# A mixture-of-experts block on one Trainium2 core: the experts' second bias added in the passes instead of by a product with the gates

## The chip, the cores and the metric

The kernel runs on one core of one Trainium2 chip. The metric is the time of one execution on the device in microseconds. Five instruction streams run side by side and meet at semaphores: TensorE (PE in the profile, its weight loads PEld), VectorE (DVE), ScalarE (ACT), GpSimd (POOL), and SyncE (SP), which here only issues DMAs.

## The reference, cut to what matters

All is float32. 1024 tokens of 1024 channels go through a mixing layer (convolution and attention), which gives `h`; then every token is sent to 4 of 32 experts:

```
v = rms_norm(h, norm2_g)
logits = v @ router_w + router_b
top_val, top_idx = lax.top_k(logits, 4)
gates = softmax(top_val)
...
def clamped_swiglu_expert(xb, w1, b1, w2, b2):
    h = xb @ w1 + b1
    x_glu = jnp.minimum(h[..., :D_FF], SWIGLU_LIMIT)
    x_lin = jnp.clip(h[..., D_FF:], -SWIGLU_LIMIT, SWIGLU_LIMIT)
    act = x_glu * jax.nn.sigmoid(SWIGLU_ALPHA * x_glu) * (x_lin + 1.0)
    return act @ w2 + b2
...
y = h + sum over the 4 experts e of a token: gate_e * expert_e(v)
```

So the second bias comes into a token's output as the sum of `gate_e * b2[e]` over its four experts.

## The kernel before, in words

**Mixing** takes the first 380 us of the span: convolution on VectorE, attention, and their projections on TensorE. It is not touched.

**Routing** goes over eight tiles of 128 tokens. Its order is written out by hand per engine, as a loop over `t` in which each engine does a piece of tile t, of tile t-1 and of tile t-2. For tile t TensorE multiplies by `w_out` in two halves (`out_half`, L1215); VectorE adds x and gets the residual tile `hb` (`residual`, L830); ScalarE squares and sums it (L596), POOL makes the root (L335, L336), and VectorE scales the tile into `vrow` (`norm_v`, L838). TensorE transposes `vrow` (L1288), ScalarE copies that (L604), TensorE multiplies by the router's weights (L1307), and VectorE picks four experts and makes the gates (`route`, L843 to L858), which stand in the last 32 columns of `vrow`. Then, two tiles behind, comes the second bias: TensorE transposes the gates (`trans_gates`, L1259), ScalarE copies them (`take_GT`, L613), TensorE multiplies them by the table of all 32 bias rows (`gates_b2`, L1269, two products of 512 columns), and VectorE adds the two halves to `hb` (`add_b2`, L864) and gives `h2_ready`. For that semaphore SP waits before it stores `hb` to the output (`store_rows`, L239), and TensorE before it reuses the banks (L1265, L1280). The row store of `vrow` to `token_rows` is issued ahead of it.

After the last tile TensorE counts ranks within experts (L1318), VectorE makes from them positions and tables (L878 to L968), and POOL gathers the tokens of the first pass from `token_rows` (`gather`, L314).

**Expert passes.** A pass has one expert and up to 256 of its token slots; there are 32 with these inputs. Passes are sorted by how many slots are filled. 18 are narrow (up to 128), then come 14 wide ones, in code of its own for each width (136, 144, 152, 176, 192 here). In `pe_pass` TensorE makes eight blocks of the hidden layer (L1001, each with its two sides), then the second layer: in a narrow pass straight into rows of tokens (`down_rows`, L1041), in a wide one transposed (`down`, L1016) and turned back (`trans_y`, L1029, L1030). Between them it transposes the next pass's tokens (`trans_x`, L1335). In `dve_pass` VectorE takes each hidden block out (`hidden_a`, L663 and L665; `hidden_b`, L672 and L675), after the second block prepares the next pass's indices, after the fourth waits for the adds of the pass before and takes over index and gate (L689, L690), and at the end takes the transposed tokens (`take_xT`, L973). The loop's head copies the expert's first bias (L655). In `act_pass` ScalarE copies the result out times the gate, in two column halves (`take_rows`, L454; `take_y`, L443 and L444), and gives `yt_ev` for each. POOL waits for both and adds the rows to the output in HBM by two indirect DMAs (`add_rows`, L320). SP loads the next weights as buffers come free: `w1` in two parts after the fourth and the eighth hidden block, `w2` in two parts after each half of the second layer (L249, L254). All weight buffers are single.

```
for c in range(2):
    sp.wait_ge(hid_mm, q * MT + (4 * c + 4 - MT))
    load_w1(sp, c, e)
for c in range(2):
    sp.wait_ge(y_mm, q * KD + (4 * c + 4 - KD))
    load_w2(sp, c, e)
```

Of the kernel before, what the change touches and what calls it, by code (L numbers as in the profile page):

```python
# [18 lines left out]
P = 128  # L19
# [20 lines left out]
HALF = 512  # L40


def hybrid_block(nc, x, norm1_g, w_in, conv_w, conv_b, conv_ln_g, conv_ln_b, q_norm_g, k_norm_g, sinks,
# [9 lines left out]
    with ExitStack() as ctx:  # L53
# [71 lines left out]
        b2_sb = part(140, D)[0:NE, :]  # L125
# [34 lines left out]
        GT = sb("GT", [NE, P])  # L160
# [54 lines left out]
        gt_mm, gt_ev, b2_mm, h2_ready = sem("gt_mm"), sem("gt_ev"), sem("b2_mm"), sem("h2_ready")  # L215
# [20 lines left out]
        def store_rows(sp, t):  # L236
            sp.wait_ge(gate_ready, t + 1)
            sp.dma_start(rows_d[t * P:(t + 1) * P, :], vrow[:, t % 2, :]).then_inc(row_out[t % 2], 16)
            sp.wait_ge(h2_ready, t + 1)  # L239
            sp.dma_start(out2[t * P:(t + 1) * P, :], hb[:, t % 4, :]).then_inc(h_out[t % 4], 16)  # L240
# [11 lines left out]
        def load_w2(sp, c, e):  # L252
            src = expert(w2, e)
            sp.dma_start(w2_sb[:, :, c * HALF:(c + 1) * HALF],  # L254
                         src[:, c * HALF:(c + 1) * HALF].rearrange("(k p) n -> p k n", p=P)).then_inc(w2_in[c], 16)

        @block.sync
        def _(sp):
# [22 lines left out]
            sp.dma_start(b2_sb, b2).then_inc(b2_in, 16)  # L281
# [10 lines left out]
            for c in range(2):  # L292
                load_w2(sp, c, 0)
            sp.wait_ge(tab_ready, 1)
            n_pass = sp.value_load(tabI[0:1, 4 * TQ:4 * TQ + 1], min_val=NE, max_val=QMAX)
            with sp.Fori(1, n_pass) as q:
# [4 lines left out]
                for c in range(2):  # L301
                    sp.wait_ge(y_mm, q * KD + (4 * c + 4 - KD))
                    load_w2(sp, c, e)

# [19 lines left out]
        def _(pool):  # L324
# [73 lines left out]
            pool.wait_ge(b2_mm, NT)  # L398
# [7 lines left out]
            with pool.Fori(0, n_pass) as q:  # L406
# [4 lines left out]
                pool.wait_ge(yt_ev, q * 2 + 2)  # L411
# [58 lines left out]
        def _(a):  # L470
# [140 lines left out]
            def take_GT(t):  # L611
                a.wait_ge(gt_mm, t + 1)
                a.activation(GT[:], bank[7][0:NE, 0:P], ACT.Copy).then_inc(gt_ev, 1)  # L613

            for t in range(NT + 1):
                if 1 <= t <= NT:
                    take_vT(t - 1)
                if t >= 2:
                    take_GT(t - 2)
# [4 lines left out]
            take_GT(NT - 1)  # L624
# [20 lines left out]
        def dve_pass(v, q, e, e_next, prep, one_hots, take_idx, take_xT):  # L645
# [55 lines left out]
            v.sem_inc(dve_loop, OWN - own[0])  # L701

        @block.vector
        def _(v):
# [155 lines left out]
            def add_b2(t):  # L860
                v.wait_ge(b2_mm, t + 1)
                for b in range(2):
                    t_ = hb[:, t % 4, b * HALF:(b + 1) * HALF]
                    last = v.tensor_tensor(t_, t_, bank[4 + b][:], ALU.add)  # L864
                last.then_inc(h2_ready, 1)

            for t in range(NT + 1):
# [5 lines left out]
                if t >= 2:  # L873
                    add_b2(t - 2)
# [31 lines left out]
            add_b2(NT - 1)  # L906
# [180 lines left out]
        def _(pe):  # L1087
# [168 lines left out]
            def trans_gates(u):  # L1256
                pe.wait_ge(gate_ready, u + 1)
                pe.wait_ge(lvar, 2)
# [138 lines left out]
```

## Time and profile before

| | |
|---|---|
| median of 3 runs | 2150.91 us (2150.83 to 2156.55) |
| the profiled execution's own time | 2154.91 us |
| its span | 2153.2 us |
| TensorE busy | 2020.3 us, 94%, in 13213 records |
| VectorE busy | 932.0 us, 43% |
| ScalarE, POOL busy | 397.5 us, 228.1 us |
| chain that ended last | TensorE 82%, VectorE 10%, issue 3%, ScalarE 2% |
| moved by DMA | 492.44 MB, 229 GB/s over the span |
| mean granted TensorE clock | 0.964 |

The own time has 1.7 us around the span. An f32 product has two records on TensorE, so "x4" of L1269 is two products. In a timeline a row is start, duration, engine, line, operation, operands, count, and in brackets how long the engine was idle before it and what released it; in the chain a row is start, length, and what stood in the chain. Durations of products overlap in the timeline, so the chain's shares are what a product takes of the time.

### The profile page before, as it was taken

Reading aid. Unit: us, or ns where it says so; the run is one execution under the profiler, and the core shown is the slowest. Engines: PE = TensorE matmul, PEld = TensorE weight load, DVE = VectorE, ACT = ScalarE, POOL = GpSimd, SP = SyncE. Lnnn points to the kernel's source line nnn. Section 1 sums busy time; section 2 is a strip of 40 time slices with the busy share of each in tenths; the row PEclk is TensorE's granted clock in tenths of the full one; section 3 lists DMA queues with packets and bytes.
Section 4 is the critical chain, followed back from the end, with each engine's and each line's share of the span. In section 5 each row is a group of like instructions: output and inputs, shape, how many; then the busy total and the mean of one; then the engine's idle time right before and its main releaser. Section 6 shows DMA issues by size and latency. Waiting matters only on the chain.

```text
span 2153.2 us, 34646 instructions
## 1 busy us (share of the span) xinstructions
PE 2020.3 (94%) x13213; PEld 1648.4 (77%) x13214; DVE 932.0 (43%) x2247; ACT 397.5 (18%) x849; POOL 228.1 (11%) x223
## 2 busy tenths in 40 slices
PE   5997887899799999999999999999999999998997
PEld 3444543444677887788878887999999999988997
DVE  2895667333444444444443444333333333333221
ACT  3113334311111111111111111121111111110111
POOL 3101110000101010011101010011000000000000
PEclk9998889998799999999999999999999999999999
DMA  5020003212599899998999899988788887775651
GB/s 224 1 78 0 1 1 134 87 66 99 195 328 336 304 327 329 337 326 305 327 338 332 298 338 328 322 286 300 275 279 275 279 280 260 267 266 166 237 176 41
DMA packets 226274, 492.44 MB, mean 229 GB/s; under 512 B 7469, under 2 KB 8009, under 8 KB 226224
## 3 DMA queue, kind: packets, MB, share of 16 engines
q1 hardware_dynamic: 207504, 431.24, 55.5%
q0 software_dynamic: 16768, 59.98, 10.2%
q8 instruction: 39, 0.64, 0.1%
q10 hardware_dynamic: 1952, 0.49, 0.1%
q14 instruction: 11, 0.09, 0.0%
HBM read 458.88 MB, written 32.80 MB: 228 GB/s over the span
## 4 chain that ended last, share of the span: by engine, by line
PE 82%; DVE 10%; issue 3%; ACT 2%; DMA 1%; POOL 1%; ACTq 0%; DVEq 0%; POOLq 0%
PE bank L1001 46%; PE bank L1041 11%; PE bank L1016 10%; DVE arena L740 5%; PE bank L1215 5%; PE bank L1335 2%; PE bank L1136 1%; PE bank L1120 1%; ACT arena L543 1%; PE bank L1269 1%; PE bank L1029 1%; DVE arena L769 1%; DVE arena L785 1%; DVE mx L774 1%; PE bank L1307 1%
## 5 line engine op out<-in xcount | busy, mean ns | idle before, releaser
L1001 PE MATMUL bank<-arena 128*128 128x128 f32 (+5 forms) x8192 | 998.4, 284 | 21.5 <-issue 21.5
L1001 PEld LDWEIGHTS bank<-arena 128*128 128x128 f32 x8192 | 989.3, 192 | 34.1 <-issue 34.1
L663 DVE TENSOR_SCALAR arena<-bank,b1c 128x256 f32<-128x256 f32 x256 | 123.8, 483 | 611.1 <-PE bank L1001 602.0
L430 ACT ACTIVATE arena<-arena 128x256 f32<-128x256 f32 x256 | 106.6, 417 | 866.7 <-DVE arena L663 784.0
L1041 PE MATMUL bank<-arena 128*128 128x512 f32 x576 | 262.1, 593 | 0.0
L1016 PE MATMUL bank<-arena 128*128 128x144 f32 (+4 forms) x1792 | 252.0, 294 | 4.6 <-DVE arena L675 4.4
L1016 PEld LDWEIGHTS bank<-arena 128*128 128x128 f32 x1792 | 237.1, 190 | 7.8 <-DVE arena L675 7.7
L973 DVE TENSOR_SCALAR arena<-bank,cols 128x256 f32<-128x256 f32 x256 | 112.1, 480 | 283.4 <-PE bank L1335 283.4
L320 POOL DMA_INDIRECT out<-arena,idx_cur x64 | 99.0, 1547 | 826.9 <-ACT arena L444 422.5
L1041 PEld LDWEIGHTS bank<-arena 128*128 128x128 f32 x576 | 102.5, 190 | 94.7 <-issue 90.4
L740 DVE SCALAR_TENSOR_TENSOR arena<-arena,cols 128x1024 f32<-128x1024 f32 x120 | 159.3, 1328 | 3.7 <-ACT arena L518 0.2
L314 POOL DMA_INDIRECT arena<-token_rows,idx_next x66 | 65.5, 992 | 630.7 <-DVE idx_next L899 551.3
L675 DVE SCALAR_TENSOR_TENSOR arena<-arena 128x256 f32<-128x256 f32 x256 | 108.9, 425 | 37.8 <-DVE arena L672 5.2
L1215 PE MATMUL bank<-arena 128*128 128x512 f32 x256 | 121.5, 631 | 3.0 <-DVE arena L822 3.0
L665 DVE TENSOR_SCALAR arena<-bank,b1c 128x256 f32<-128x256 f32 x256 | 121.6, 475 | 0.0
L1120 PE MATMUL bank<-arena 128*128 128x512 f32 x256 | 110.2, 592 | 0.0
L672 DVE TENSOR_TENSOR arena<-arena 128x256 f32<-128x256 f32 x256 | 106.3, 415 | 0.0
L1215 PEld LDWEIGHTS bank<-arena 128*128 128x128 f32 x256 | 50.6, 202 | 67.7 <-issue 63.9
L1120 PEld LDWEIGHTS bank<-arena 128*128 128x128 f32 x256 | 48.5, 190 | 60.3 <-issue 60.3
L1335 PEld LDWEIGHTS bank<-ident,arena 128*128 128x128 f32 x392 | 50.5, 144 | 42.7 <-issue 33.7
L434 ACT ACTIVATE arena<-bank 128x256 f32<-128x256 f32 x112 | 42.9, 383 | 211.3 <-PE bank L1016 211.3
L1335 PE MATMUL bank<-ident,arena 128*128 128x128 f32 x392 | 66.4, 279 | 3.3 <-ACT arena L631 2.9
(222 smaller groups left out, 1108.8 us busy)
## 6 DMA issues: line engine op xcount, KB each, us to landing
arena<-in_w SPq DMA_DIRECT2D x192, 2048.0 KB, 11.9
arena<-in_x SPq DMA_DIRECT2D x16, 512.0 KB, 5.2
token_rows<-arena SPq DMA_DIRECT2D x8, 528.0 KB, 5.9
arena<-in_w_in SPq DMA_DIRECT2D x2, 2048.0 KB, 11.2
out<-arena SPq DMA_DIRECT2D x8, 512.0 KB, 2.9
arena<-in_w_in SPq DMA_DIRECT2D x1, 3072.0 KB, 23.3
arena<-in_w_out SPq DMA_DIRECT2D x1, 2048.0 KB, 9.5
arena<-in_w_out SPq DMA_DIRECT2D x2, 1024.0 KB, 15.6
```

Source lines behind the costliest of these rows:

```text
L430: a.activation(sg[:, m % 2, :], g1[:, m % 2, :], ACT.Sigmoid, scale=ALPHA).then_inc(sg_ready, 1)
L663: v.tensor_scalar(g1[:, r, :], bank[r][:, 0:SLOTS], b1c[:, m:m + 1], LIMIT, ALU.add, ALU.min).then_inc(g1_ready, 1)
L665: v.tensor_scalar(l1[:, r, :], bank[r][:, SLOTS:], b1c[:, MT + m:MT + m + 1], LIMIT + 1.0, ALU.add, ALU.min).then_inc(hid_free, 1)
L675: v.scalar_tensor_tensor(act[:, m, :], l1[:, r, :], 1.0 - LIMIT, tt[:, r, :], ALU.max, ALU.mult).then_inc(act_ready, 1)
L740: link(v.scalar_tensor_tensor(cT[:, c, :], zT[:, c, j:j + SEQ], col(CW + c * WIDTH + j), cT[:, c, :], ALU.mult, ALU.add))
L973: last = v.tensor_scalar(xT[:, k, :], bank[6][:, (k % 2) * SLOTS:(k % 2 + 1) * SLOTS], col(G2 + k), None, ALU.mult)
L1001: last = mm(bank[m % 2][:, side * SLOTS:side * SLOTS + n], w1_sb[:, k, lo:lo + P], xT[:, k, 0:n], start=k == 0, stop=k == KD - 1)
L1016: last = mm(bank[2 + d % 2][:, 0:n], w2_sb[:, m, d * P:(d + 1) * P], act[:, m, 0:n], start=m == 0, stop=m == MT - 1)
L1041: last = mm(bank[4 + b][:], act[:, m, 0:P], w2_sb[:, m, b * HALF:(b + 1) * HALF], start=m == 0, stop=m == MT - 1)
L1120: last = mm(bank[2 * (i % 2) + side][:], w_cv[:, k, lo:lo + P], uT[:, k, h * HALF:(h + 1) * HALF], start=k == 0, stop=k == KD - 1)
L1215: last = mm(bank[mixed_bank(t) + b][:], src, w_o[:, k, b * HALF:(b + 1) * HALF], start=part_ == 0 and i == 0, stop=part_ == 1 and i == CT - 1)
L1335: last = pe.transpose(bank[6][:, (k % 2) * SLOTS + h * P:(k % 2) * SLOTS + (h + 1) * P], gath[:, h, k * P:(k + 1) * P], ident[:])
```

## The change

The gates' transposes, their copies, the products with the bias table and the adds to `hb` are removed. In each pass SP loads the expert's row of `b2` into all 128 partitions (0.52 MB in SBUF from 4 KB in HBM), and VectorE adds gate times that row to the gated result, after ScalarE's copy: four operations of 512 columns, two token halves by two column halves. `y_ready` takes the place of `yt_ev` in POOL's wait, and SP waits for it before it overwrites the row. The residual tile is stored as soon as it is made, ahead of the row store.

```diff
-        b2_sb = part(140, D)[0:NE, :]
+        b2_rows = part(160, D)
...
         def store_rows(sp, t):
+            sp.wait_ge(h_ready, t + 1)
+            sp.dma_start(out2[t * P:(t + 1) * P, :], hb[:, t % 4, :]).then_inc(h_out[t % 4], 16)
             sp.wait_ge(gate_ready, t + 1)
             sp.dma_start(rows_d[t * P:(t + 1) * P, :], vrow[:, t % 2, :]).then_inc(row_out[t % 2], 16)
-            sp.wait_ge(h2_ready, t + 1)
-            sp.dma_start(out2[t * P:(t + 1) * P, :], hb[:, t % 4, :]).then_inc(h_out[t % 4], 16)
...
+        def load_b2(sp, e):
+            src = b2[e:e + 1, :] if isinstance(e, int) else b2[ds(e, 1), :]
+            sp.dma_start(b2_rows, src.to_broadcast([P, D])).then_inc(b2_in, 16)
...
             sp.wait_ge(var_mm, 2)
-            sp.dma_start(b2_sb, b2).then_inc(b2_in, 16)
...
             for c in range(2):
                 load_w2(sp, c, 0)
+            load_b2(sp, 0)
...
                     sp.wait_ge(y_mm, q * KD + (4 * c + 4 - KD))
                     load_w2(sp, c, e)
+                sp.wait_ge(y_ready, q)
+                load_b2(sp, e)
...
-            pool.wait_ge(b2_mm, NT)
...
                 gather(pool, q + 2)
-                pool.wait_ge(yt_ev, q * 2 + 2)
+                pool.wait_ge(y_ready, q + 1)
...
-                if t >= 2:
-                    take_GT(t - 2)
...
                 take_xT(q4, i)
             v.sem_inc(dve_loop, OWN - own[0])
+            v.wait_ge(b2_in, q * 16 + 16)
+            for b in range(2):
+                v.wait_ge(yt_ev, q * 2 + b + 1)
+                for h in range(2):
+                    y = ytok[:, h, b * HALF:(b + 1) * HALF]
+                    last = v.scalar_tensor_tensor(y, b2_rows[:, b * HALF:(b + 1) * HALF], gate_cur[:, h:h + 1], y,
+                                                  ALU.mult, ALU.add)
+            last.then_inc(y_ready, 1)
...
-                if t >= 2:
-                    add_b2(t - 2)
...
-            add_b2(NT - 1)
...
-                    if u >= 2:
-                        pe.wait_ge(h2_ready, u - 1)
...
-                if t >= 2:
-                    trans_gates(t - 2)
...
-                if t >= 2:
-                    gates_b2(t - 2)
...
-            trans_gates(NT - 1)
-            gates_b2(NT - 1)
...
-            pe.wait_ge(h2_ready, NT)
```

On TensorE the last steps of the routing loop, before (the `w_out` products L1215, `vrow`'s transposes L1288, the gates' L1259, the router's L1307, the bias's L1269, the ranks' L1318):

```order
L1215 MATMUL bank<-arena 128x512 x8
L1259 MATMUL bank<-ident,arena 32x128
L1307 MATMUL bank<-rw,arena 128x32 x8
L1269 MATMUL bank<-arena,GT 128x512 x2
L1288 MATMUL bank<-ident,arena 128x128 x8
L1259 MATMUL bank<-ident,arena 32x128
L1307 MATMUL bank<-rw,arena 128x32 x8
L1269 MATMUL bank<-arena,GT 128x512 x2
L1318 MATMUL bank<-Mb,tri_b 128x32
```

And the same place in the change, whose line numbers are lower (L1210 is `w_out`, L1265 the transposes, L1282 the router, L1291 the ranks):

```order
L1210 MATMUL bank<-arena 128x512 x8
L1282 MATMUL bank<-rw,arena 128x32 x8
L1265 MATMUL bank<-ident,arena 128x128 x8
L1282 MATMUL bank<-rw,arena 128x32 x8
L1291 MATMUL bank<-Mb,tri_b 128x32
```

Nothing is left on TensorE between the router's products of one step and the next piece of work; each of the steps before them lost the same two entries.

On VectorE the end of the pass loop, before (the last tokens' L973, then the loop's branch):

```order
L971 REGISTER_ALU
L973 TENSOR_SCALAR arena<-bank,cols 128x256 x2
L983 REGISTER_ALU
L983 COMPARE_AND_BRANCH
```

In the change (L968 is the last tokens', L704 the bias, with a wait at L701 ahead of each pair):

```order
L968 TENSOR_SCALAR arena<-bank,cols 128x256 x2
L701 ISA
L704 SCALAR_TENSOR_TENSOR arena<-arena,gate_cur 128x512 x2
L701 REGISTER_ALU
L704 SCALAR_TENSOR_TENSOR arena<-arena,gate_cur 128x512 x2
L978 REGISTER_ALU
L978 COMPARE_AND_BRANCH
```

The two pairs stand between the last tokens and the branch to the next pass, so the loop's head follows them.

On SP the end of its pass loop in the change (L253 loads `w2`, L258 the bias row):

```order
L253 DMA arena<-in_w 128x8x512
L258 ISA
L258 DMA arena<-in_b 128x1024
L299 REGISTER_ALU
L299 COMPARE_AND_BRANCH
```

The wait and the load come behind the last part of `w2` and ahead of the next pass's `w1`.

## Rows read from the trace of the kernel before

**Rows 1.** The page, DMA busy in tenths in 40 slices of the span

```profile
DMA  5020003212599899998999899988788887775651
```

**Rows 2.** The chain of waits, routing stage: start, length, what

```profile
417.60 0.11 PE bank L1259
...
419.42 1.91 PE bank L1269 x4
...
517.16 2.41 PE bank L1269 x4
519.57 3.71 issue
523.29 1.96 PE bank L1288 x8
...
529.54 3.72 PE bank L1269 x4
...
533.28 1.29 DVE arena L864 x2
...
542.90 6.17 DMA arena<-token_rows,idx_next
```

**Rows 3.** Timeline, end of the routing stage, VectorE and SP

```profile
518.20 0.75 DVE L838 TENSOR_SCALAR arena<-arena,rs 128x1024 f32<-128x1024 f32 x1 [2.12 <-POOL rs L336]
...
521.90 1.28 DVE L864 TENSOR_TENSOR arena<-arena,bank 128x512 f32<-128x512 f32 x2
...
531.73 0.18 DVE L853 CAST Mb<-Mf 128x32 bf16<-128x32 f32 x1
...
541.55 0.34 SPq L240 DMA_DIRECT2D out<-arena  x1
```

**Rows 4.** Timeline, two halves of L1215, and a window (busy times, PEclk, DMA share, GB/s)

```profile
429.10 7.03 PE L1215 MATMUL bank<-arena 128*128 128x512 f32 x16
...
439.79 8.83 PE L1215 MATMUL bank<-arena 128*128 128x512 f32 x16
...
441.00:442.00 1.00, 1.00 (x2) 0.37 (x2) 0.89 (x5) 0.00 (x0) 0.00 (x0) 0.50 0.00 0
```

**Rows 5.** Timeline, the narrow pass that begins at 957.08: VectorE, ScalarE, POOL

```profile
955.51 0.17 DVE L655 COPY b1c<-b1T 128x16 f32 x1 [0.78 <-issue]
960.86 0.48 DVE L663 TENSOR_SCALAR arena<-bank,b1c 128x256 f32<-128x256 f32 x1 [5.17 <-PE bank L1001]
...
964.43 0.48 DVE L663 TENSOR_SCALAR arena<-bank,b1c 128x256 f32<-128x256 f32 x1 [2.70 <-PE bank L1001]
...
973.27 0.16 DVE L689 COPY idx_cur<-idx_next 128x2 int32<-128x2 int32 x1
...
957.37 0.69 ACT L454 ACTIVATE arena<-bank,gate_cur 128x512 f32<-128x512 f32 x1 [6.42 <-PE bank L1041]
...
960.95 1.38 POOL L320 DMA_INDIRECT out<-arena,idx_cur  x1 [0.30 <-issue]
```

**Rows 6.** The instructions of L740: duration in ns, min/median/max

```profile
L740 DVE SCALAR_TENSOR_TENSOR arena<-arena,cols x120: 1273/1285/2173, 64.2 to 340.6; 128x1024 f32<-128x1024 f32 x120
```

**Rows 7.** DMA: issues (KB, us to landing), landing of L320, window of one narrow pass

```profile
arena<-in_w SPq DMA_DIRECT2D x192, 2048.0 KB, 11.9
arena<-in_x SPq DMA_DIRECT2D x16, 512.0 KB, 5.2
...
DMA to landing us min/median/max: 7.2/7.4/9.3
...
957.08:1000.77 43.69, 43.69 (x313) 35.83 (x312) 19.02 (x54) 5.99 (x11) 4.99 (x4) 1.00 0.92 324
```

**Rows 8.** Timeline, a wide pass, and the switch to the 176-wide code

```profile
1823.80 0.68 ACT L444 ACTIVATE arena<-bank,gate_cur 128x512 f32<-128x512 f32 x1
...
1827.93 0.48 DVE L663 TENSOR_SCALAR arena<-bank,b1c 128x256 f32<-128x256 f32 x1 [5.84 <-PE bank L1001]
...
1943.22 7.08 PE L1001 MATMUL bank<-arena 128*128 128x176 f32 x28 [10.01 <-issue]
```

More of the change, by code:

```diff
@@ L159, in hybrid_block @@
         gs = sb("gs", [P, 4])
-        GT = sb("GT", [NE, P])
         Mb = sb("Mb", [P, NT, NE], bf16)
@@ L214, in hybrid_block @@
             "vt_mm", "vt_ev", "lg_mm", "lg_neg", "eg_ready", "gate_ready", "mask_ready"))
-        gt_mm, gt_ev, b2_mm, h2_ready = sem("gt_mm"), sem("gt_ev"), sem("b2_mm"), sem("h2_ready")
+        y_ready = sem("y_ready")
         row_out = [sem(f"row_out{i}") for i in range(2)]
@@ L609, in gate_exp @@
                 a.activation(eg[:], lg[:], ACT.Exp, bias=gs[:, 0:1]).then_inc(eg_ready, 1)
-            def take_GT(t):
-                a.wait_ge(gt_mm, t + 1)
-                a.activation(GT[:], bank[7][0:NE, 0:P], ACT.Copy).then_inc(gt_ev, 1)
             for t in range(NT + 1):
@@ L623, in _ @@
                     gate_exp(t - 1)
-            take_GT(NT - 1)
             for i in range(2):
@@ L858, in route @@
                 v.tensor_scalar(vrow[:, t % 2, D:ROW], gg[:], gs[:, 2:3], None, ALU.mult).then_inc(gate_ready, 1)
[L860 to L865, printed above, removed]
             for t in range(NT + 1):
@@ L1254, in _ @@
             out_half(2, 0)
-            def trans_gates(u):
-                pe.wait_ge(gate_ready, u + 1)
-                pe.wait_ge(lvar, 2)
-                pe.transpose(bank[7][0:NE, 0:P], vrow[:, u % 2, D:ROW], ident[:]).then_inc(gt_mm, 1)
-            def gates_b2(u):
-                if u == 0:
-                    pe.wait_ge(b2_in, 16)
-                else:
-                    pe.wait_ge(h2_ready, u)
-                pe.wait_ge(vt_ev, 2 * min(u + 2, NT))
-                pe.wait_ge(gt_ev, u + 1)
-                for b in range(2):
-                    last = mm(bank[4 + b][:], GT[:], b2_sb[:, b * HALF:(b + 1) * HALF], start=True, stop=True)
-                last.then_inc(b2_mm, 1)
             for t in range(NT + 1):
```

## The prediction

> **What bounds the kernel now.** I read the page first, then the chain of waits, then the timeline of every engine at three places: the eight routed token tiles, one narrow expert pass and one wide one. The DMA slices are at 8 or 9 tenths in nearly the whole expert stage [rows 1]: that asks whether a pass waits for its weights, and it is the first thing to settle, since the change adds transfers there. In the routing stage the chain is TensorE's own work almost without a gap, and the products with the transposed gates (L1269) and their transposes (L1259) stand in it [rows 2]. In the passes it is TensorE again: in a narrow pass VectorE and ScalarE sit idle between their pieces, each waiting for TensorE [rows 5]. So what leaves TensorE in the routing stage is worth its full time, and what VectorE, POOL and the DMA get in the passes costs nothing until it is late for TensorE.
>
> **The change, part by part.**
>
> *Routing stage, steps with five tiles.* Each had a gate transpose (0.11 in the chain) and four records of L1269, which are two f32 products, at 1.91 us; the row at 419.42 stands for the five from 419 to 500 [rows 2]. 5 x 1.91 = 9.6, and six transposes at 0.11 = 0.7: **10.2 us saved**. TensorE stays the bound in a shortened step: the next thing it needs is the normalised tile, and that was ready 1.8 us after L1269 began (518.95 against 517.16 [rows 2, 3]), while in these steps 7 us of L1215 come before it is asked for [rows 4].
>
> *The last steps.* After the sixth pair (517.16, 2.41) TensorE stood 3.71 us, until 523.29 [rows 2]. The normalised tile was ready at 518.20 + 0.75 = 518.95; what TensorE stood for was the wait on h2_ready, given by VectorE's L864 at 521.90 + 1.28 = 523.18 [rows 3]. Both waits go, so the transposes can start at 519.0: 523.3 - 519.0 = **4.3 us saved**, and what is late next is VectorE's L838. Then the pair at 529.54 (3.72) ends at 533.26 [rows 2] while the mask that the rank products wait for (L853) is ready at 531.91 [rows 3]; L864 (533.28, 1.29) ran beside those products. Both gone: 1.35, less a handover, **1.2 us saved**. The eighth pair lay beside VectorE's rank arithmetic, and is worth nothing; so are ScalarE's eight copies of the gates.
>
> *Stores and first gather.* The residual tile is now stored as soon as it is made, before its row store. The gather of the first pass is in the chain with 6.17 us [rows 2], and the last residual store was issued at 541.55, just ahead of it [rows 3]. That store is 0.52 MB; at the 324 GB/s of a pass [rows 7] it takes 1.6. Bounds 0 and 1.6, because the gather's own start-up may have hidden it; I take **0.6 saved**, nearer the lower end, since the store had begun earlier.
>
> *VectorE in the passes.* Four new operations per pass, 128 in all. No row has 128x512 of this form; L740 has it at 1285 ns for 1024 columns [rows 6], so 0.64 to 0.69 each, I take 0.66, with 84 us in all on VectorE. The first pair of a pass runs when TensorE still multiplies. The second waits for the last gated copy, which in the narrow pass ends at 957.37 + 0.69 = 958.06 [rows 5]; the pair ends at 959.4, and the loop's head (0.78 and 0.17 at L655) moves behind it, to 960.35. VectorE's next work came at 960.86, when TensorE's first block was ready, and TensorE needs the result only for its third block, near 964.4 [rows 5]. So 0.5 us are left before anything moves, and some 3 before TensorE does. In the wide pass the copy ends at 1824.48, the pair and the head at 1826.8, and the work comes at 1827.93 [rows 8]. **Cost 0**, cover TensorE's first block; every us beyond the 3 would be paid in each of 31 passes.
> The Trainium skill (Vector Engine (DVE) Microarchitecture Reference, "Points that are easy to get wrong") says this form with two sources in SBUF that aren't bf16 halves throughput. The row of L740 has both sources f32 in SBUF and stands at one column in 1.25 ns, so I don't double it. By that rule, as an estimate, a pair would take 2.6: hidden in the passes, and 1.3 more at the end.
>
> *POOL.* Its adds to the output now wait for y_ready, 1.3 us later. The second was issued at 960.95 and lands 7.4 us on, at most 9.3 [rows 5, 7]; so 969.7 now, or 971.6. VectorE asks for it at 973.27 [rows 5]. Behind POOL's wait there are only the adds and the next pass's gather, which waits for VectorE's words after 973.27 anyway. Cost 0.
>
> *SP and DMA.* The load of the bias row waits for y_ready (959.4) behind the w2 loads; behind it on SP is the next w1 load, which waits for TensorE's fourth block (about 972) anyway. The load is 0.52 MB. Its time on the 16 DMA engines isn't in the trace. Lower end 1.6 us, at the pass's 324 GB/s; upper end 5.2, what a tile of x of that size took from issue to landing [rows 7]. I take 1.6, since transfers queue behind each other here and a latency isn't occupancy. The narrow pass has the engines at 0.92 of 43.7 us: 3.5 us free [rows 7]. It fits, and **costs 0** in 18 narrow passes; the 14 wide ones are longer with the same weights.
> At one place it may not be free: the switch to the 176-wide code, where TensorE stood 10.01 us with nothing recorded [rows 8] while the w2 load ran; I read it as code coming through the same DMA engines. The new load may add to it: 0 to 1.6, I take **0.8 lost**.
>
> *End.* The last add starts a pair later: **1.3 lost**, nothing covers it.
>
> *The clock.* In three of the five steps TensorE's granted clock fell to 0.50, its lower level of 1.2 GHz, for some 3 us, after the stretch of L1307 and L1269, with TensorE busy the whole time; an L1215 group then took 8.83 where 7.03 is usual, 1.8 each, 5.3 in all [rows 4]. The change takes half of that stretch away. Bounds: all 5.3 back, or none and two more falls (-3.6). I take **4.0 saved**, nearer the first, because in two steps of before the same stretch passed without a fall, so it is near the edge.
> The Trainium skill (TensorE: Matmul & The Clock Gate, "Why this matters for your kernels") ties the fall to idle gaps of TensorE. The row shows it at full busy share, so the trace disagrees. By that rule this term would be 0, and the time 4 us higher.
>
> *Sum:* 10.2 + 4.3 + 1.2 + 0.6 - 0.8 - 1.3 = 14.2, and 4.0 of clock: 18.2. Against the profiled execution's own 2154.91 this gives 2136.7; the runs' median is 2150.91, 4.0 lower, from which it would be 2132.7. I can't tell which of the two had the usual number of falls of the clock, so I go between: **2135**.
>
> **The rivals.**
> *The clock falls as often as before* (22 in 100). For it: each step still has the short products of L1307 and eight transposes. 14.2 saved: 2154.9 - 14.2 = 2140.7, or 2136.7 from the median; 2139.
> *A switch of code waits longer* (7 in 100). Its 10.01 stands beside others of a fraction of that, so it isn't stable, and TensorE's code moves in memory. If a second switch gets such a gap, or this one grows by the same: 2135 + 10 = 2145, which counts as no change.
> *The same, shorter* (6 in 100). If it falls to the 1 or 2 us of a plain switch: 2135 - 8 = 2127.
> *The broadcast load is slow: slower than before* (5 in 100). All 128 partitions read one 4 KB row. If the load holds the engines for e us, narrow passes become bound by DMA once e is above the free 3.5, first eating the lead that w1 has over TensorE (its 4 MB are asked for at 972 and needed when the next pass begins at 1000.77, and 11.9 us to landing [rows 7] leave about 16). The gain is gone at 18(e - 3.5) = 16 + 16, e = 5.3; at e = 8 it is 81 - 16 = 65 us lost: 2200. Against it: 5.2 for a whole landing of that size.
> *VectorE comes late: slower too* (3 in 100). It decides when the second pair and the head take more than 3 us above my 2.3. At 1 us beyond that, 31 us: 2166.
>
> **How the numbers follow.** My forecast has 57 in 100. Measurement can tell 0.3%, 6.5 us, from no change: the border is at 2144.4. Forecast, usual clock falls and the shorter switch lie below it: 0.85. The longer switch and the upper edge of the others: 0.08. Slower: 0.07. Range: best ends of the terms from the median, 2150.9 - 21.3 = 2129.6, widened to 2127 for the shorter switch; worst ends from the profiled time, 2154.9 - 12.7 + 3.6 = 2145.8, so 2146. What it leaves out is the two slower cases and part of the switch.
>
> **What would show it.** Right: no idle of TensorE between the routed tiles, a wait of some 1.8 us for L838 at the end, the first expert block about 20 us earlier, narrow passes of still 43.7 us, the new VectorE operations near 0.66 and done before the next block, adds landing before VectorE asks, a tail 1.3 longer. Wrong: idle of TensorE ahead of its first or third block, narrow passes longer than 43.7, a bias load that lands after the pass ends, L1215 groups of 8.8 still there.

## The result, and the profile after

Median 2132.43 us of 4 runs (2128.89 to 2135.2), against 2151.4 of before in the same comparison: ratio 0.9886, 95% interval 0.9865 to 0.9908. The ratio makes the saving 24.5 us, and its interval 20 to 29; the two medians are 19.0 apart. The prediction of 2135 against 2150.91 had 15.9. The 2132.4 lies inside the range of 2127 to 2146 and the sign is right, but by the ratio the 2150.91 of before would become 2126.4, just under that range: the saving is larger than predicted. The ratio is not that of the two medians (0.9912), and the record doesn't show the runs that make up the rest of it. In a second comparison (e10 below) the ratio made the saving 19.8, interval 15.7 to 23.9. Both intervals hold 20 to 24. One execution of e9 (2656.24 us) and one of e10 (7463.63) were in a far slower state; the ratios leave them out, the medians count them (2155.95 and 2136.81 without them).

The profiled execution took 2132.26, 22.65 less than that of before. From its page:

```profile
PE 1994.0 (94%) x13173; PEld 1638.9 (77%) x13174; DVE 1009.8 (47%) x2359; ACT 395.5 (19%) x841; POOL 228.1 (11%) x223
...
DMA  6020002332699999999999999899888887885651
...
L704 DVE SCALAR_TENSOR_TENSOR arena<-arena,gate_cur 128x512 f32<-128x512 f32 x128 | 90.3, 747 | 65.9 <-ACT arena L458 36.8
```

TensorE is busy 26.3 us less than in the table of before, VectorE 77.8 more, and the time still followed TensorE. The DMA slices are as full as in [rows 1].

**Where the 22.65 went**, each from the same place in both traces:

| stretch | before | after | gain |
|---|---|---|---|
| start of the span to L1259 (after: L1282) of the first of five full steps | 417.60 | 419.20 | -1.6 |
| the five steps, to the end of the last `w_out` half | 97.75 | 81.99 | 15.8 |
| from there to the end of the ranks' products (L1318, after: L1291) | 19.2 | 13.7 | 5.5 |
| from there to the first expert block | 27.0 | 26.0 | 1.05 |
| first block to the switch to the 176-wide code | 1371.6 | 1370.0 | 1.7 |
| the gap at the switch | 10.01 | 9.46 | 0.5 |
| the rest of the passes | 196.1 | 195.6 | 0.5 |
| after TensorE's last instruction | 13.9 | 14.75 | -0.9 |

The chain of waits of after, routing stage (start, length, what). L1210 is `w_out`, L1265 the transposes, L1282 the router's products, L843 the normalised tile, L858 the mask, L1291 the ranks:

```profile
419.20 1.71 PE bank L1282 x16
420.90 6.95 PE bank L1210 x16
427.85 0.87 PE bank L1265 x8
428.73 6.87 PE bank L1210 x16
435.59 1.70 PE bank L1282 x16
...
494.31 6.88 PE bank L1210 x16
501.21 0.70 DVE arena L835
...
504.03 0.77 DVE arena L843
504.84 1.91 PE bank L1265 x8
506.77 0.61 ACT arena L608
507.42 3.64 PE bank L1282 x16
...
513.24 0.19 DVE Mb L858
513.48 1.37 PE bank L1291 x44
...
523.21 5.23 DMA arena<-token_rows,idx_next
```

A step is now 16.4 us (435.59 - 419.20), with no idle time in it; the 1.91 of the bias products is gone from each, and every half of L1210 takes 6.9. In before, three of the five halves right behind L1269 took 8.83 ([rows 4] has one). At the end TensorE waits for L843 instead of the 3.71 of [rows 2], then for the mask: what the prediction put next (it had 1.8 us of waiting for L838, and TensorE's timeline shows 1.96 for L843). The gather, once 6.17 [rows 2], takes 5.23.

The five steps as a window in the trace of before, then of after (us, busy times, PEclk, DMA share, GB/s):

```profile
417.60:515.35 97.75, 97.75 (x308) 49.00 (x307) 29.90 (x100) 14.11 (x30) 3.69 (x10) 0.95 0.25 82
```

```profile
419.20:501.19 81.99, 81.99 (x283) 43.53 (x282) 23.98 (x90) 12.78 (x25) 3.69 (x10) 1.00 0.28 95
```

TensorE is fully busy in both, and the granted clock goes from 0.95 to 1.00: the falls in this stretch are gone. Of the 15.8 us, 10.1 are the removed products and transposes (five times 1.91 and 0.11 in the chain), 5.1 are three falls (8.76 where a half behind L1269 otherwise takes 7.06), and 0.5 is the rest: without a fall that half takes 7.06 behind L1269 and 6.95 behind the router's products.

A narrow pass of after, timeline of all engines (compare [rows 5]): L704 is the bias, L652 the loop's head, L660 the first work on a hidden block, L325 the adds, L258 the load of the bias row:

```profile
936.84 0.69 ACT L458 ACTIVATE arena<-bank,gate_cur 128x512 f32<-128x512 f32 x1 [6.42 <-PE bank L1036]
937.56 1.41 DVE L704 SCALAR_TENSOR_TENSOR arena<-arena,gate_cur 128x512 f32<-128x512 f32 x2 [2.04 <-ACT arena L458]
939.31 0.18 DVE L652 COPY b1c<-b1T 128x16 f32 x1 [0.34 <-issue]
940.33 0.48 DVE L660 TENSOR_SCALAR arena<-bank,b1c 128x256 f32<-128x256 f32 x1 [0.84 <-PE bank L996]
...
952.74 0.16 DVE L686 COPY idx_cur<-idx_next 128x2 int32<-128x2 int32 x1
...
939.14 0.34 SPq L258 DMA_DIRECT2D arena<-in_b  x1
...
939.92 1.63 POOL L325 DMA_INDIRECT out<-arena,idx_cur  x1 [23.32 <-DVE arena L704]
941.87 1.38 POOL L325 DMA_INDIRECT out<-arena,idx_cur  x1 [0.31 <-issue]
...
936.55 14.45 PE L996 MATMUL bank<-arena 128*128 128x128 f32 x128
```

The second pair starts as soon as ScalarE's copy ends and is done at 938.97. The head follows at once, and VectorE still waits 0.84 for TensorE's first block. The second add is issued at 941.87 and lands 8.5 later (median; 10.6 at most, which would be 952.47), so before 952.74, when VectorE asks for it. The window of that pass, beside [rows 7]:

```profile
936.55:980.24 43.69, 43.69 (x314) 35.84 (x312) 21.77 (x58) 5.99 (x11) 4.99 (x4) 1.00 0.95 337
```

43.69 us as before, and TensorE busy for all of it. The DMA share rose from 0.92 to 0.95.

### The profile page after: what moved, and what is told of

The parts are those of the page before. It is cut to its first block, busy times and chain, and to the rows that moved or that the text cites. A ratio compares the mean times of both kernels' runs of the same rounds, so it can differ in the third digit from the quotient of the medians.

```text
span 2130.6 us, 34778 instructions
## 1 busy us (share of the span) xinstructions
PE 1994.0 (94%) x13173; PEld 1638.9 (77%) x13174; DVE 1009.8 (47%) x2359; ACT 395.5 (19%) x841; POOL 228.1 (11%) x223
## 3 DMA queue, kind: packets, MB, share of 16 engines
q0 software_dynamic: 16768, 59.98, 10.2%
## 4 chain that ended last, share of the span: by engine, by line
PE 82%; DVE 10%; issue 3%; ACT 2%; DMA 1%; POOL 1%; ACTq 0%; DVEq 0%; POOLq 0%
PE bank L996 46%; PE bank L1036 12%; PE bank L1011 10%; DVE arena L745 5%; PE bank L1210 4%; PE bank L1308 2%; PE bank L1131 1%; PE bank L1115 1%; ACT arena L547 1%; PE bank L1024 1%; DVE arena L774 1%; DVE arena L790 1%; DVE mx L779 1%; PE bank L1299 1%; PE bank L1025 1%
## 5 line engine op out<-in xcount | busy, mean ns | idle before, releaser
L996 PE MATMUL bank<-arena 128*128 128x128 f32 (+5 forms) x8192 | 996.6, 284 | 20.5 <-issue 20.5
L996 PEld LDWEIGHTS bank<-arena 128*128 128x128 f32 x8192 | 987.5, 192 | 33.1 <-issue 33.1
L660 DVE TENSOR_SCALAR arena<-bank,b1c 128x256 f32<-128x256 f32 x256 | 123.8, 484 | 472.9 <-PE bank L996 472.9
L968 DVE TENSOR_SCALAR arena<-bank,cols 128x256 f32<-128x256 f32 x256 | 112.1, 480 | 283.4 <-PE bank L1308 283.4
L325 POOL DMA_INDIRECT out<-arena,idx_cur x64 | 99.0, 1547 | 873.3 <-DVE arena L704 863.5
L662 DVE TENSOR_SCALAR arena<-bank,b1c 128x256 f32<-128x256 f32 x256 | 121.7, 475 | 0.0
L704 DVE SCALAR_TENSOR_TENSOR arena<-arena,gate_cur 128x512 f32<-128x512 f32 x128 | 90.3, 747 | 65.9 <-ACT arena L458 36.8
L1210 PE MATMUL bank<-arena 128*128 128x512 f32 x256 | 117.8, 616 | 3.0 <-DVE arena L827 3.0
L1210 PEld LDWEIGHTS bank<-arena 128*128 128x128 f32 x256 | 49.5, 198 | 61.4 <-issue 57.6
## 6 DMA issues: line engine op xcount, KB each, us to landing
arena<-in_b SPq DMA_DIRECT2D x32, 512.0 KB, 10.9
```

What stands on the lines that cost most here:

```text
L660: v.tensor_scalar(g1[:, r, :], bank[r][:, 0:SLOTS], b1c[:, m:m + 1], LIMIT, ALU.add, ALU.min).then_inc(g1_ready, 1)
L662: v.tensor_scalar(l1[:, r, :], bank[r][:, SLOTS:], b1c[:, MT + m:MT + m + 1], LIMIT + 1.0, ALU.add, ALU.min).then_inc(hid_free, 1)
L968: last = v.tensor_scalar(xT[:, k, :], bank[6][:, (k % 2) * SLOTS:(k % 2 + 1) * SLOTS], col(G2 + k), None, ALU.mult)
L996: last = mm(bank[m % 2][:, side * SLOTS:side * SLOTS + n], w1_sb[:, k, lo:lo + P], xT[:, k, 0:n], start=k == 0, stop=k == KD - 1)
L1210: last = mm(bank[mixed_bank(t) + b][:], src, w_o[:, k, b * HALF:(b + 1) * HALF], start=part_ == 0 and i == 0, stop=part_ == 1 and i == CT - 1)
```

## The experiments

The theory after this reading: the passes cost nothing, and the gain is all in the routing stage, partly as clock. The rivals: the passes gave or took something after all (the loads, VectorE's margin, the adds' wait), or the clock's share was luck of one execution. Ratios are against before, on the same chip; before's medians there were 2155.4 to 2158.3, of 13 to 17 runs. Lines added to a kernel move its line numbers by a few.

### Do the passes cost anything: e1, e2

e1 is after without the second bias:

```diff
-                load_b2(sp, e)
...
-                pool.wait_ge(y_ready, q + 1)
+                pool.wait_ge(yt_ev, q * 2 + 2)
...
-                    last = v.scalar_tensor_tensor(y, b2_rows[:, b * HALF:(b + 1) * HALF], gate_cur[:, h:h + 1], y,
-                                                  ALU.mult, ALU.add)
```

> The changed kernel without anything of the second bias in the passes: no load of its row, no VectorE operation, POOL waits for yt_ev again. It leaves the second bias out altogether. My theory: the passes hide all of it but the tail, so this is the change's routing part alone and lies 1.3 to 1.5 us below the changed kernel, at about 2131, with narrow passes of 43.7 us in both. The rival, that the passes pay for VectorE's work or the load a little each, would show as 10 us or more below the changed kernel.

e2 is the other half alone: before, with the loads, the four operations and POOL's wait in the passes, and the products with the gates kept.

```diff
+                sp.wait_ge(y_ready, q)
+                load_b2(sp, e)
...
-                pool.wait_ge(yt_ev, q * 2 + 2)
+                pool.wait_ge(y_ready, q + 1)
...
+                    last = v.scalar_tensor_tensor(y, b2_rows[:, b * HALF:(b + 1) * HALF], gate_cur[:, h:h + 1], y,
+                                                  ALU.mult, ALU.add)
```

> The kernel before, with its products with the gates, and with the change's pass part added: the load, the four VectorE operations and POOL's wait. It adds the second bias twice. My theory: 1.3 to 2 us over the kernel before, so about 2152.5, and three falls of TensorE's clock in the routing loop as before. If the gain came in part from the passes, this would be faster than the kernel before.

Measured: e1 2133.31, ratio 0.9879 (0.9856 to 0.9902); e2 2156.97 in 10 runs, ratio 1.0000 (0.9985 to 1.0014). Taking the pass work out of after gains nothing, putting it into before loses nothing. The narrow pass of e1:

```profile
937.06:980.75 43.69, 43.69 (x314) 35.83 (x313) 19.04 (x54) 5.99 (x11) 4.99 (x4) 1.00 0.91 324
```

Same length, 2.7 us less of VectorE, and DMA at 0.91. So the gain is the routing stage's, and the pass side of the change is free within 3 us in 2150. The end of the span is too short a piece to be seen in these medians; it is read from the traces.

### How near VectorE is to being late: e3, e4

Three or eight more operations of the same form behind the second pair, into unused memory:

```diff
+            for i in range(3):
+                last = v.scalar_tensor_tensor(part(164 + 2 * i, HALF), b2_rows[:, 0:HALF], gate_cur[:, 0:1],
+                                              b2_rows[:, HALF:], ALU.mult, ALU.add)
```

(e4: `range(8)`.)

> The changed kernel with three more operations of the same form on VectorE after the second pair, into unused memory. They take about 2.1 us. My theory of the margin (TensorE needs VectorE's first block only for its third, some 3 us after the loop's head ends): TensorE isn't held up, only the tail is 2.1 later: about 2134.5. The rival, that VectorE's first block must be on time as before, has only 0.5 us of room: 1.5 to 2 us in each of 31 passes, 2180 to 2195.

> The same with eight more operations, about 5.5 us. My theory: some 2.5 us beyond the margin in a narrow pass and 1.5 in a wide one, so TensorE idle ahead of its third block in each, 31 passes: 50 to 85 us slower, about 2200. If VectorE doesn't matter at all it stays at 2138.

e3 came to 2136.97, ratio 0.9904 (0.9888 to 0.9921): its interval meets that of after. In its VectorE timeline the head comes right behind the added three, and the first block's work without a wait:

```profile
939.42 1.42 DVE L704 SCALAR_TENSOR_TENSOR arena<-arena,gate_cur 128x512 f32<-128x512 f32 x2 [2.04 <-ACT arena L458]
940.75 2.07 DVE L707 SCALAR_TENSOR_TENSOR arena<-arena,gate_cur 128x512 f32<-128x512 f32 x3
942.74 0.17 DVE L652 COPY b1c<-b1T 128x16 f32 x1
943.05 0.48 DVE L660 TENSOR_SCALAR arena<-bank,b1c 128x256 f32<-128x256 f32 x1
```

TensorE went from its second block to its third without a gap. VectorE may be late for the first block, so long as it is not late for the third.

e4 came to 2183.13, ratio 1.0119 (1.0102 to 1.0136), at the low end of what was expected. TensorE's timeline and its group in e4 (L999 is the block, L662 the operation that frees its bank):

```profile
905.47 7.31 PE L999 MATMUL bank<-arena 128*128 128x128 f32 x64
914.35 7.41 PE L999 MATMUL bank<-arena 128*128 128x128 f32 x64 [1.57 <-DVE arena L662]
```

```profile
L999 PE MATMUL bank<-arena 128*128 128x128 f32 (+5 forms) x8192 | 1007.2, 285 | 54.7 <-DVE arena L662 35.0 <-issue 19.6
```

Two blocks run (64 records), then TensorE stands 1.57 us for VectorE, in each narrow pass; 35.0 us over 26 places. The whole is 50 us above after; besides the 35.0 the blocks themselves take 10.6 more (1007.2 against 996.6 for after's L996), and the end behind TensorE's last instruction grew from 14.75 to 20.3. The narrow pass goes from 43.69 to 45.52 (914.35 to 959.88, the next third block). This is the rival "VectorE comes late" as written, with its place right, and its point: eight operations at 0.69 (2.07 / 3) are 5.5 us, less the 3.95 that didn't show (5.52 - 1.57). By the length of the pass it is 5.52 less 1.83. So the margin beyond the second pair is 3.7 to 4.0 us, where the prediction had "some 3".

### What the broadcast load costs: e5

Four loads per pass instead of one, three of them into unused memory:

```diff
-            sp.dma_start(b2_rows, src.to_broadcast([P, D])).then_inc(b2_in, 16)
+            for i in range(4):
+                dst = b2_rows if i == 0 else part(160 + 4 * i, D)
+                sp.dma_start(dst, src.to_broadcast([P, D])).then_inc(b2_in, 16)
...
-            v.wait_ge(b2_in, q * 16 + 16)
+            v.wait_ge(b2_in, q * 64 + 64)
```

> The changed kernel with four broadcast loads of the bias row per pass in place of one (the other three into unused memory; VectorE waits for all). My price is 1.6 us of the DMA engines for each, so 4.8 more per pass: with 3.5 free of which the first load took 1.6, the narrow passes would need 46.6 us of DMA against 43.7: after the lead of about 16 us is used up, TensorE waits, at most 18 x 2.9 - 16 = 36 us in all: 2132 to 2168. If a load costs 5.2 of the engines, the narrow passes would be 15 us longer each: over 2300. If it is far cheaper than 1.6 (1.2 or less), nothing moves: 2133.

Measured 2131.57, ratio 0.9887 (0.9855 to 0.9919): no loss at four. The window of a narrow pass of e5:

```profile
936.34:980.03 43.69, 43.69 (x313) 35.82 (x312) 21.75 (x58) 5.99 (x11) 4.99 (x4) 1.00 1.04 373
```

and its DMA issues (KB each, us to landing):

```profile
arena<-in_w SPq DMA_DIRECT2D x192, 2048.0 KB, 14.6
arena<-in_b SPq DMA_DIRECT2D x128, 512.0 KB, 12.2
```

The share goes 0.91 (no load, e1), 0.95 (one), 1.04 (four; as it can go above 1, this figure isn't a limit by itself). From one to four loads it is 0.09 x 43.7 / 3 = 1.3 us a load; from none to one 0.04 x 43.7 = 1.7. Rates rise along: 324, 337, 373 GB/s. So 1.3 to 1.7 us of the 16 engines, where the prediction took 1.6 and feared 5.2, and the rival "slow broadcast load" falls by a wide margin: four together hold the engines for 7 us at most, and even then the pass waits for nothing. The weights land later (14.6 where [rows 7] has 11.9), inside their lead.

### The clock: e6, e7, e9, e10

In e6 the two products of 32 rows by 512 columns are put back six times, with nothing that waits for them; five of the six have a `w_out` half right behind them; in e7 the same with 128 rows.

```diff
+                    if 1 <= u <= NT - 2:
+                        for b in range(2):
+                            mm(bank[7][:], w_o[0:32, 0, 0:P], w_o[0:32, 0, b * HALF:(b + 1) * HALF],
+                               start=True, stop=True)
```

(e7: `w_o[0:128, ...]` for both.)

> The changed kernel with the two products of 32 rows and 512 columns put back behind the router's in six steps of the routing loop, on constant operands and into an unused bank, without transposes, copies, adds or waits. It computes the same as the changed kernel. TensorE's own time: 6 x 1.91 = 11.5 us more. My theory of the clock: the falls come from the stretch of the router's products and these, so they return in some of the steps, 1.8 each: 2144 to 2150. The rival, that the falls came with the waits or by chance, gives 2143.9 and no window at 0.50 between the routed tiles.

> The same with products of 128 rows, so with the whole array in use: the same 1.91 us each. If the few rows matter for the clock, no falls here where the kernel with 32 rows has them: 2143.9, and up to 5 us between the two. If only the time of the stretch matters, both have the same number of falls.

e6: 2148.93, ratio 0.9957 (0.994 to 0.9974). e7: 2141.74, ratio 0.9924 (0.9898 to 0.9949). The two do the same number of products of the same columns, and 7.2 us lie between the medians. The intervals just overlap (0.994 to 0.9949). But the mean granted clock over the whole span was 0.965 to 0.968 in every one of e6's ten runs and 0.969 to 0.972 in every one of e7's six. Three windows of e6, each where its granted clock was down:

```profile
444.60:448.00 3.40, 3.40 (x5) 1.35 (x4) 2.36 (x13) 0.32 (x1) 0.00 (x0) 0.50 0.00 0
465.10:468.50 3.40, 3.40 (x5) 1.35 (x4) 2.02 (x10) 0.13 (x1) 0.00 (x0) 0.50 0.08 35
502.60:506.00 3.40, 3.40 (x5) 1.45 (x5) 2.95 (x16) 0.32 (x1) 0.00 (x0) 0.50 0.00 0
```

and the whole stretch of e7 (its 0.99 comes from a fall that ends at 417.6, ahead of the first of its five steps at 422.71; e6 has one at the same place):

```profile
415.00:520.00 105.00, 104.04 (x352) 54.63 (x351) 29.73 (x114) 15.33 (x31) 4.43 (x12) 0.99 0.26 86
```

In e6 TensorE is busy throughout and the clock is at 0.50, its 1.2 GHz, as in [rows 4]; in e7 it stays at its 2.4 GHz between the tiles. The L1210 halves say the same. In e6:

```profile
444.18 8.83 PE L1210 MATMUL bank<-arena 128*128 128x512 f32 x16
453.72 7.03 PE L1210 MATMUL bank<-arena 128*128 128x512 f32 x16
464.30 8.83 PE L1210 MATMUL bank<-arena 128*128 128x512 f32 x16
```

and in e7 every one of the ten takes 7.03. So it was the bias products that brought the falls, by the few rows they use, and not their time, nor L1282's products and the transposes beside them, which all three kernels have.

The five steps take 97.14 us in e6 and 90.57 in e7. Some 5 of the 6.6 between them are the falls. The rest is 0.3 a step (18.42 against 18.11 without a fall): the pair of 32 rows and the half behind it take a little longer by themselves. After's step takes 16.40, so a pair of 128 rows costs 1.7 and one of 32 rows 2.0. The first block of e7 starts 10.5 us later than after's (551.31 against 540.84), but that isn't the price of the products alone: 3.7 came ahead of the steps, 8.6 in them, and 1.8 were regained behind them, where the clock fell only at 520.4.

The prediction set the rule of the Trainium skill (TensorE: Matmul & The Clock Gate, "Why this matters for your kernels"), that falls follow idle gaps of TensorE, against [rows 4]. By that rule e6 and e7 would be equal, since neither has a gap between the tiles. The runs disagree with it for these products of few rows. The trace agrees with it for the long fall at the end of routing, which begins behind an idle stretch of 1.96 us and lasts while TensorE is busy for less than half of the time, in after:

```profile
505.00:546.00 41.00, 18.69 (x128) 15.63 (x128) 20.46 (x100) 6.47 (x13) 5.87 (x5) 0.50 0.50 182
```

e9 and e10 are before and after unchanged, run again, since one profile doesn't say what is usual.

> The kernel before once more, for its clock. The comparison of the change gave 0.9886, 24 us, while the medians first shown lie 19 apart and my sum is 18.2. My theory: the falls of TensorE's clock between the routed tiles vary from run to run in the kernel before, and the profiled execution had few: ratio 1.00, a spread of 8 us or more among its runs, and 3 to 6 falls of 3.4 us between 400 and 500 us in this profile.

> The changed kernel once more on the same chip. My theory: no fall between the tiles from 410 to 500 us, a narrower spread than the kernel before, and a ratio of 0.987 to 0.991. If the spread is as wide as that of the kernel before, the falls aren't what varies.

e9: 2156.21, ratio 1.0008 (0.9993 to 1.0023). e10: 2137.08, ratio 0.9908 (0.9889 to 0.9927). The first profile of before had three falls in the five steps and one just ahead of them; so had e2's and e9's, with the third of double length. One long L1215 half of e9:

```profile
480.55 10.02 PE L1215 MATMUL bank<-arena 128*128 128x512 f32 x16
```

10.02 where 8.83 was the worst before. Nine profiles have the change and no bias products beside it (after, e1, e3, e4, e5, e8, e10, e11, e12): none has a fall between 420 and 500 us. So the falls are usual in before and absent in after, and the first profile of before was an ordinary execution, with rather few. The spreads don't settle it: 17 runs of before on this chip lie within 13 us and five of after within 8, but the four of e1, which has no bias products at all, within 9.6.

### The gap at the switch of code: e8

TensorE stands 9.46 us before the 176-wide code [rows 8 has 10.01], and 1.7 at the other changes of width. There the next code follows in memory, while here the code for 160 slots, which no pass uses, lies between and is skipped. The second half of the `w2` load is in flight then. e8 holds that half back until the next pass's first block is done:

```diff
-                    sp.wait_ge(y_mm, q * KD + (4 * c + 4 - KD))
+                    if c == 0:
+                        sp.wait_ge(y_mm, q * KD + (4 - KD))
+                    else:
+                        sp.wait_ge(hid_mm, q * MT + 1)
```

> The changed kernel with SP's load of the second part of w2 waiting for the next pass's first hidden block, some 4 us later. My reading of TensorE's 9.5 us gap at the switch to the 176-wide code: its code comes through the DMA engines behind that load. Then the gap falls to the 1.7 us of the other switches, and with the load needed only 38 us later nothing else moves: 2132.4 - 7.8 = 2124.6. The rival, that the gap is something of the switch itself, leaves it at 9.5 and the time at 2132.

Measured 2132.72, ratio 0.9893 (0.9864 to 0.9921), so the 2124.6 didn't come. The gap went to 6.18, and not to 1.7:

```profile
1910.89 0.27 PE L1028 MATMUL bank<-ident,arena 128*128 128x128 f32 x1
1917.34 21.99 PE L999 MATMUL bank<-arena 128*128 128x176 f32 x128 [6.18 <-issue]
```

A window of the DMA queues inside the gap, of after (first) and of e8: packets, MB, share of the 16 engines.

```profile
q1 hardware_dynamic: 598, 1.42, 67.4%
q0 software_dynamic: 61, 0.25, 27.2%
q8 instruction: 1, 0.02, 1.2%
```

```profile
q0 software_dynamic: 16, 0.07, 20.8%
q8 instruction: 2, 0.03, 3.3%
```

In after the instruction packet falls in 1914.8 to 1920.3, some 4 us after TensorE ran dry at 1910.8, with 1.42 MB of loads around it; in e8 the first falls in 1912.5 to 1917.4, 1.4 us after, on idle engines. So 3.3 us of the gap went with the queue of loads, of which 2.6 are seen in the packet's place, and 6.2 are the switch itself. That the packet is TensorE's code is my reading; the view doesn't say whose it is. The gap was 8.5 to 10.3 in the twelve profiles with the early load, 6.18 and 5.73 in the two with the late one (e8, e12). In the total, 3.3 us can't be told from the scatter of the runs. The new load of the bias row was issued at 1913.72 in after, in the middle of the gap, and still the gap is no longer than before (9.46 against 10.01; e1, without that load, has 10.28, e2, with it, 9.70, e5, with four, 8.65): the 0.8 that the sum charged for it isn't there.

### Can it be bettered: e11, e12

The clock is down from 505.0 to 546.0 of after, while TensorE waits in pieces. e11 adds 21 products nobody reads (128 rows, 512 columns, into bank 7) at six places where it waits; e12 adds e8's edit.

```diff
+            def warm(n):
+                for i in range(n):
+                    mm(bank[7][:], ident[:], b1T[:], start=True, stop=True)
```

> The changed kernel with 21 idle products of 128 rows and 512 columns on TensorE, on constant operands into an unused bank, put where TensorE waits between the last routed tile and the first pass. My theory: the granted clock stays at 1.00 there, and what TensorE does on the chain there at 0.50 (transposes 1.91 for 1.04, router 3.64 for 1.87, first block of the first pass 16.97 for 14.5, four groups of token transposes) takes half: 6 to 9 us faster than the changed kernel, about 2125. The rival, that idle products arrive late and hold up the chain, gives 0 to 5 us slower.

> The same together with the later load of the second part of w2, which took the gap at the switch of code from 9.46 to 6.18 us: 3 us below e11, about 2122, faster than both kernels. If the later load delays w1 instead, it is no faster than e11.

e11: 2132.67, ratio 0.9877 (0.9857 to 0.9897), beside e10's 2137.08 on the same chip. e12: 2131.57, ratio 0.9885 (0.9866 to 0.9904), gap at the switch 5.73. Neither came near what was expected, 2125 and 2122. The chain of e11:

```profile
512.62 1.99 PE bank L1288 x16
...
531.79 0.67 PE bank L1315 x4
```

and its window up to 536.9:

```profile
413.00:536.90 123.90, 115.67 (x464) 62.23 (x464) 49.12 (x205) 21.83 (x43) 11.08 (x19) 1.00 0.32 106
```

The granted clock stays at full level through the waits up to 536.9; there it falls once, until 540.9, just ahead of the first block. In e12, with the same 21 products, it fell twice, from 507 to 512 and from 528 to 536. So these products shorten the fall and don't reliably prevent it. The last router products (L1288) take 1.99 instead of 3.64, the token transposes 0.67 instead of 1.13. From the end of the last `w_out` half to the first block it is 36.9 us (505.73 to 542.63) against 39.65 in after, and the first block itself takes 14.55 instead of 16.97: some 5 us in the trace. The intervals of e11 and e10 overlap (0.9889 to 0.9897), and 2132.67 is no less than after's first 2132.43, so a better version than after is possible, and not shown.

## Why the prediction was right, and where it was wrong

**What bounds the kernel, and the passes: right.** TensorE was the bound, the passes cost nothing (e1, e2), and each reason held: the second pair hidden beside the first block, the adds landed in time, the load small. Its sizes: L704 at 747 ns where 0.66 was taken, from a row with twice the columns: the two rows together make it 1.05 ns a column and 209 ns fixed, and halving a row of 1024 columns halved the fixed part too. The head behind the pair took 0.34 and not 0.78 of idle, and evened that out. The rule of the Trainium skill (Vector Engine (DVE) Microarchitecture Reference, "Points that are easy to get wrong") that this form halves throughput would, as an estimate against L740's rate, make a pair 2.6. It took 1.41, so the trace disagrees with that reading; the page doesn't say which rate is halved.

**The routing terms: right to 0.5 us each.** Products and transposes 10.2 predicted; a step of before without a fall takes 18.53 (417.60 to 436.13) against 16.40, which is 10.7 in five. The 0.5 too little is the `w_out` half behind the products, which the sum put at nothing. The waits for `h2_ready` and the mask, 4.3 + 1.2 predicted, 5.5 measured. Stores and gather 0.6 predicted, 1.05 measured, the gather alone 0.9.

**The clock: the mechanism right, the size too small.** "I take 4.0 saved": in the two profiles it was 5.1 in the steps. (The 5.3 set 8.83 against 7.03, a second half of `w_out`; a first half without a fall takes 7.13, so a fall costs 1.7.) 1.6 were given back before the steps, and one fall in an expert block of before (L1001 at 1766.76 took 18.47, the same block in after 16.80) was worth 1.7 more. Nothing in the traces ties that last one to the change: nine of the fourteen profiles have one near there, with and without the bias products. That before had it and after not is luck, in favour of the change. Why the stretch ahead of the steps took 1.6 longer isn't explained either: the clock fell there twice for 6.8 us in after, once for 6.8 and once for 3.4 in before.

**The step that failed: the size of the saving, and with it the range's lower end.** "2150.9 - 21.3 = 2129.6", widened to 2127, rests on 21.3 as the most that the terms could give, and 18.2 as their sum. The two profiles lie 22.65 apart, and the first comparison's ratio makes the saving 24.5. The 4.4 between 18.2 and 22.65, term by term: in the steps 1.6 (clock 1.1, the half behind the products 0.5), the fall in the expert block 1.7, the switch 1.3 (0.5 gained for 0.8 lost), the gather 0.45, the tail 0.4, the rest of the passes 0.5, less the 1.6 given back ahead of the steps. So the clock was mis-sized (4.0 for 5.1), the switch was charged for something that isn't there, and the clock outside the steps was put at nothing. From 22.65 to 24.5 the cause stays open: no trace covers it, and the second comparison has 19.8.

**The base failed beside it.** "I can't tell which of the two had the usual number of falls of the clock, so I go between." The forecast thus started from 2153.2 (2135 + 18.2), about half-way between the profiled 2154.91 and the median 2150.91 of three runs, and was set against the lower one: 18.2 became 15.9 by that choice alone. In later comparisons on three chips, with 13 to 17 runs of before each, the median is 2155.4 to 2158.3, and the profiles of e2 and e9 show the falls that the first one shows: the profiled execution was ordinary and two of the three runs lay low. Whether by fewer falls or by their chip isn't shown, as they left no trace. From 2154.91 the sum gives 2136.7, and the profiled execution of after is at 2132.26. That the forecast of 2135 is only 2.6 us from the measured 2132.43 is therefore in part luck: a saving too small was taken from a base that was higher than the one it is compared with.

**Small terms.** 0.8 lost at the switch: not there; the gap is 0.5 shorter, and e8 shows what it is made of. Tail 1.3 predicted, 0.9 measured.

The rival "the clock falls as often as before" is refuted by after, e1 and e10. The two rivals on the gap didn't come. Of the slower ones, VectorE coming late is a real mechanism with more room than thought (e4); the slow load didn't show even with four loads (e5).

## What to carry to other kernels

Work taken off the engine that is the bound and put where a trace shows idle time ahead of a known deadline was worth its full time here; work out the deadline from the rows (here the third block, not the first) and the new place is free until then. Where a granted clock falls with TensorE fully busy, look at how many rows the products just before it use: here the pair of 32-row products cost its own 1.9 us in every step and 1.7 more in clock in three of five. And where the clock falls now and then, a term of clock and the base belong together: state the sum against the execution whose falls were counted.

## What was unexpected of the hardware

- Same count, same columns: products of 32 rows brought three falls of the clock in five steps, products of 128 rows none (e6, e7, one profile each), 7.2 us apart in the medians, with TensorE at full busy share in both.
- A switch to code that isn't next in memory held TensorE 5.7 to 6.2 us on an idle DMA (e8, e12) and 8.5 to 10.3 under load, against 1.7 where the code follows on. The Trainium skill (Runtime: NRT & Kernel Launch, "Instruction fetch mechanics") says that a taken branch out of the engine's small window of code makes it fetch the target by DMA before it goes on; the packets of q8 in the gap agree. The page gives no time for it, and in after the one packet in the gap came 5 us before TensorE started.
- A broadcast of one 4 KB row into 128 partitions, 0.52 MB in all, is no slower than the same bytes of weights: 1.3 to 1.7 us of the engines; 10.9 from issue to landing, as median. That it queues behind `w2` would explain this, but isn't shown.
